# Two of the sixteen query weight tiles stay in SBUF, and the ring of gathered rows has eight slots in place of ten

## What is computed

```python
def block(xb):                                     # 128 tokens of 1024 values
    qh = (xb @ wq).reshape(128, 8, 2, 128)         # wq is 1024 x 2048
    s1 = einsum('thd,nd->thn', qh[:, :, 0], keys1)
    s2 = einsum('thd,nd->thn', qh[:, :, 1], keys2)
    v1, i1 = top_k(s1, 16); v2, i2 = top_k(s2, 16)
    cand = (v1[..., :, None] + v2[..., None, :]).reshape(128, 8, 256)
    sc, ci = top_k(cand, 16)
    e = take(i1, ci // 16) * 128 + take(i2, ci % 16)          # 128 tokens x 8 heads x 16 experts
    act = gelu(einsum('td,thkd->thk', xb, u_tab[e])) * softmax(sc)
    return einsum('thk,thkd->td', act, v_tab[e])
```

## Time and profile before

| | |
|---|---|
| median of 3 runs | 3160.18 us (3155.35 to 3163.76) |
| the profiled execution | 3159.13 us, its span 3157.3 us |
| PE busy | 2576.8 us (82%) |
| DVE busy | 2196.9 us (70%) |
| POOL busy | 1999.2 us (63%) |
| ACT busy | 691.8 us (22%) |
| DMA | 1212.72 MB in all, mean 384 GB/s; 1107.43 MB by the queue of the gathers, 102.80 MB by SP's |
| gathers | 1056 U, 1056 V (32 of them for the sample tokens) |

### The profile page before, as it was taken

The page is one execution under the profiler, slowest core; times in us unless marked ns, Lnnn a source line. Parts: engine busy times, 40 slices in busy tenths (PEclk is TensorE's granted clock), DMA queues, the critical chain, the costliest instruction groups (busy, mean ns, idle before and its releaser), DMA issues.

```text
span 3157.3 us, 39117 instructions
## 1 busy us (share of the span) xinstructions
PE 2576.8 (82%) x11988; PEld 1169.1 (37%) x11988; DVE 2196.9 (70%) x5635; ACT 691.8 (22%) x2526; POOL 1999.2 (63%) x2131
## 2 busy tenths in 40 slices
PE   7787989878987888778987888778987888777666
PEld 2553444234522453234522453234422453233111
DVE  2363887579856887579756987678756987678553
ACT  2121122112311122112311222112311232111112
POOL 0131667765777567765777567765777567766775
PEclk9888999878987899879987999878987999877566
DMA  7453999999999999999999999999999999999998
GB/s 268 136 205 116 411 387 405 419 419 385 404 413 419 416 384 419 419 419 385 412 415 419 410 388 414 419 416 368 418 412 419 414 387 414 419 419 378 417 419 356
DMA packets 339981, 1212.72 MB, mean 384 GB/s; under 512 B 41064, under 2 KB 41200, under 8 KB 339776
## 3 DMA queue, kind: packets, MB, share of 16 engines
q0 software_dynamic: 304128, 1107.43, 87.7%
q1 hardware_dynamic: 35648, 102.80, 8.4%
HBM read 1205.21 MB, written 4.87 MB: 383 GB/s over the span
## 4 chain that ended last, share of the span: by engine, by line
PE 33%; DMA 24%; DVE 22%; issue 11%; POOL 7%; ACT 3%; POOLq 0%; SPq 0%; DVEq 0%; ACTq 0%
PE bank L486 19%; DMA ring<-peer_v,idxv 17%; PE acc L486 14%; DVE ring L1496 8%; DMA ring<-peer_u,idx 7%; POOL ring L462 7%; DVE kw L1277 1%; DVE idxv L1329 1%; ACT xn L902 1%; DVE kw L1302 1%; DVE kw L1304 1%; DVE topi L1279 1%; DVE eh L1306 1%; DVE tops L1278 1%; DVE topi L1280 1%
## 5 line engine op out<-in xcount | busy, mean ns | idle before, releaser
L1496 DVE SCALAR_TENSOR_TENSOR ring<-ring,xcur 128x1024 f32<-128x1024 f32 x1056 | 1282.6, 1218 | 603.6 <-DMA ring<-peer_u,idx 596.7
L486 PE MATMUL acc<-ring,wv 128*32 128x512 f32 x4224 | 1304.9, 712 | 462.1 <-DMA ring<-peer_v,idxv 319.3
L462 POOL DMA_INDIRECT ring<-peer_u,idx x1056 | 1000.7, 948 | 685.7 <-issue 401.0
L462 POOL DMA_INDIRECT ring<-peer_v,idxv x1024 | 965.1, 942 | 409.4 <-issue 267.7
L486 PEld LDWEIGHTS acc<-ring,wv 128*32 128x32 f32 x4224 | 172.1, 115 | 1098.0 <-DMA ring<-peer_v,idxv 776.4
L486 PEld LDWEIGHTS bank<-xT,win 128*128 128x128 f32 (+1 forms) x2304 | 262.6, 182 | 104.7 <-issue 99.8
L486 PE MATMUL bank<-xT,win 128*128 128x128 f32 (+1 forms) x2304 | 293.0, 282 | 3.7 <-ACT xT L902 2.4
L902 ACT ACTIVATE wv<-rep,coefv 128x32 f32<-128x32 f32 x1024 | 264.4, 311 | 76.4 <-PE acc L486 74.5
L486 PE MATMUL bank<-win,xT 128*128 128x512 f32 (+3 forms) x368 | 184.0, 634 | 1.9 <-ACT xT L902 1.9
L486 PEld LDWEIGHTS bank<-xT,qk 128*128 128x128 f32 x1024 | 154.6, 239 | 65.6 <-issue 65.6
L486 PE MATMUL bank<-xT,qk 128*128 128x128 f32 x1024 | 167.8, 331 | 0.0
(11 more groups left out here) (231 smaller groups left out, 2181.5 us busy)
## 6 DMA issues: line engine op xcount, KB each, us to landing
qk<-wq SPq DMA_DIRECT2D x64, 512.0 KB, 6.6
t<-wq SPq DMA_DIRECT2D x64, 512.0 KB, 6.6
ring<-peer_u,idx POOLq DMA_INDIRECT x1056, 7.3
ring<-peer_v,idxv POOLq DMA_INDIRECT x1024, 7.2
win<-w_in SPq DMA_DIRECT2D x6, 2048.0 KB, 15.0
ring<-wq SPq DMA_DIRECT2D x16, 512.0 KB, 5.3
wout<-w_out SPq DMA_DIRECT2D x1, 4096.0 KB, 21.3
xn<-x_prompt SPq DMA_DIRECT2D x8, 512.0 KB, 8.4
```

The source lines that it names most:

```text
L462: pool.indirect_dma_start(out=ring[:, slot, :], out_offset=None, in_=(peer_u, peer_v)[which], in_offset=bass.IndirectOffsetOnAxis(ap=rows_ ...
L486: return nc.tensor.matmul(out, lhsT, rhs, start=start, stop=stop)
L1496: stt(row, row, 1.0, xcur[:, :], ALU.mult, ALU.mult, accum_out=dots[:, column(b, e):column(b, e) + 1]).then_inc(s_dot, 1)
```

## The change

Tiles 14 and 15 of `wq`, those of the last head, are loaded once, at the start, into a new tile `wq_kept`, and stay there. In the blocks SP loads tiles 0 to 13 alone. The new tile takes 8 KB of each partition, which are the two slots by which the ring is shorter.

```diff
-RING = 10
+RING = 8
+KEPT = 2
...
+        wq_kept = sb("wq_kept", [P, KEPT, CM, P])
...
             for ft in range(QUERY_SLOTS):
                 sp.dma_start(wq_s(ft), wq[ft]).then_inc(s_wq_s[ft], 16)
+            for half in range(KEPT):
+                sp.dma_start(wq_kept[:, half, :, :], wq[2 * PEER_HEADS - KEPT + half]).then_inc(s_wq_kept, 16)
             store_states(0, 0, 0)
...
             for b in range(BLOCKS - 1):
                 load_wq(b, range(12, 14))
                 load_x(b + 1, x_prompt[b * P + P:b * P + 2 * P, :])
-                load_wq(b, range(14, 16))
                 load_wq(b + 1, range(12))
                 store_y(b, y_prompt[b * P:b * P + P, :])
-            load_wq(BLOCKS - 1, range(12, 16))
+            load_wq(BLOCKS - 1, range(12, 14))
...
-                    pe.wait_ge(s_wq[half], b * 128 + 16 * head + 16)
+                    if ft >= 2 * PEER_HEADS - KEPT:
+                        pe.wait_ge(s_wq_kept, 16 * KEPT)
+                        tile = wq_kept[:, half, :, :]
+                    else:
+                        pe.wait_ge(s_wq[half], b * 16 * (PEER_HEADS - 1) + 16 * head + 16)
+                        tile = wq_buf[half]
                     for c in range(CM):
-                        last = mm(bank[2 + half][:, 0:P], wq_buf[half][:, c, :], xT[:, c, :], start=c == 0, stop=c == CM - 1)
+                        last = mm(bank[2 + half][:, 0:P], tile[:, c, :], xT[:, c, :], start=c == 0, stop=c == CM - 1)
```

More of the change, by code:

```diff
@@ L192, in program @@
         s_x = sem("s_x")
+        s_wq_kept = sem("s_wq_kept")
         s_wq = [sem("s_wq0"), sem("s_wq1")]
```

## The result

The changed kernel takes 3242.97 us in the median (3229.64 to 3249.95, 4 runs), before 3161.97 us (4 runs). The ratio is 1.0248, 95% interval 1.0229 to 1.0267: 81 us slower, where 40 were forecast. The profiled execution took 3240.89 us, its span 3239.1 us.

A forecast was written before the change was run, and what follows sets the result against it. Transfers were taken as the limit except in the heads, where DVE is. Terms of 2.5, 1.6 and 1.2 us made 5.3 a block, 37 for seven blocks, plus 2.5 for the last: 40 us slower, 3200 us, range 3162 to 3238.

The forecast's parts named there:

- The sign and the main mechanism: Whole kernel: 1.3% slower, since the shorter ring costs time and the removed loads give nothing back.
- The removed loads: Two loads fewer in each of eight blocks, before stretches with spare DMA time: taken as 0, bounds 0 and -20.0 us.
- A pause of POOL there can't be made good afterwards.: Away from weight loads, POOL back to back offers 423 GB/s, hardly more than the DMA engines take.
- the transfers are the limit outside the head slices: Outside the dips once a block, DMA engines nine tenths busy or more were read as the limit.
- The queue of 1.3 us: Gathers land 7.3 us after issue, 6.0 after a pause; the difference, queued transfers, covers that much of a pause.
- Term 1: End of each block's head: ring full behind DVE, then transfers limit; two slots fewer cost the full price, 2.5 us.
- Term 2: Mid-block stretch at 1943: PE's mixer piece makes POOL pause; eight slots lose 2.4 us, 1.6 more than ten.
- Term 3: Pauses ten slots hide wholly, as before 2086.18 and in the mixer: 1.2 us a block, bounds 0 and 7.5.
- The half price: Hidden pauses were charged half of one full price, 1.2 us a block, since weight loads lie beside them.
- The last block: Final block, without a mixer: only the end of its head costs, 2.5 us.
- the engines hang on each other: Rival: a late PE starves DVE in the head too; five places, 12.5 us a block, 100 us, 3260 us; chance 0.10.
- The checks named ahead: Changed profile: 7.3 MB less, waits above 417 us, landing under 7.3 us, 377 GB/s, loads near 360 us apart, deeper dips.

The follow-up runs named there:

- e2: Kernel before with ten slots, tiles 14 and 15 not loaded in the blocks: 3162.52 us, ratio 1.0006.
- e10: Kernel before with eight slots and no query weights loaded in the blocks, PE using columns of w_in instead: 3200.35 us, ratio 1.0113.
- e9: Kernel before, ten slots kept, with no query weights loaded in the blocks, PE using columns of w_in instead: 3118.68 us, ratio 0.9858.
- e1: Kernel before with eight slots instead of ten, all query weight tiles still loaded: 3249.34 us, ratio 1.0271.
- e3: Kernel before with its ten slots dealt by kind, four for U rows and six for V rows: 3202.54 us, ratio 1.0132.
- e5: Changed kernel with ACT making the V rows' weights up to three ticks earlier within each group of 16: 3234.52 us, ratio 1.0236.
- e8: Kernel before with seven slots instead of ten, all loads made: 3384.16 us, ratio 1.0714.

## Why the prediction was half right

**The sign and the main mechanism.** Both were right: the ring costs, the loads give nothing. The size was wrong: the measured 3243 us lie just outside the range of 3162 to 3238 us, twice as far from before as forecast.

**The removed loads, taken as 0.** Right. e2 shows it with the rest of the change left out.

**"A pause of POOL there can't be made good afterwards."** Right, and the main reading of the earlier trace rows: POOL's 1.24 us a gather leave no margin. e10 shows the price nearly unchanged (82 us for 90) with the loads gone. But the sentence before it, that the transfers are the limit outside the head slices, was too strong: e9 gets back 43 of 160 us. The busy share of nine tenths in the earlier trace rows doesn't tell POOL's pace from the engines' own. The queue of 1.3 us was read too small: the 6.0 us of the earlier trace rows are a median over 26 us of gathers, not the time after a pause. Of the gathers that went out after a pause of over 4 us in the trace of before, three have a landing on record: 4.1 to 4.3 us, all in the first 260 us of the kernel. A longer queue would cover more of a pause, so this error made the forecast larger, not smaller; it isn't what failed.

**Term 1, the end of the head, 2.5 us.** Right in size and place: 2.5 in the changed kernel, e1 and e3.

**Term 2, the stretch at 1943, 1.6 us.** Wrong in place: eight slots lose 0.1 us there, and the stretch 51 us later in the changed kernel has 414 GB/s, not fewer than 403. The pause at 1945.19 belonged to a short turn. It stands before the U gather of tick 82, which takes over the slot of a V, the ninth gather before it, and so waits for PE (`s_vsum`), though the trace puts its wait down to DVE. With eight slots no turn is short, and the U gather of tick 82 waits for a dot: its pause is 0.0 us in the mean where it was 1.2. Pauses of V gathers from tick 80 to 86, 0.9 us in all where there were 0.1, took its place. I had looked for pauses that were visible with ten slots and not asked which slot the gather waited for.

**Term 3, the pauses that ten slots hide, 1.2 us.** This is the step that failed, by its size. Measured is the rest of the block: 10.1 - 2.5 = 7.6 us for terms 2 and 3 together, 9.7 in e1, against 2.8 foreseen; the place of term 2 has 0.2 of it. The upper bound that I gave for this term alone, 7.5 us for three places at full price, would have been the right value. The half price rested on the loads of the weights lying beside these pauses. But the dearest stage, from tick 58 (1892 to 1932 us in the block shown), has no load beside it, and that from 98 (1996 to 2037 us) two, at 2028.8 and 2033.7. And the loads don't make pauses good: with none of them, in e10 against e9, eight slots cost 82 us where they cost 90 with them, and the stage from 98 costs 0.8 us without loads and 2.2 with them. The one pause that the term named, the 4.22 us before 2086.18, is a V gather's behind the first row of a group; its stage, from 130, loses nothing (-0.1). What the term should have counted is in the sorted table: POOL's pauses outside the head rise by 8.9 us a block, 3.7 of them behind DVE, 2.4 behind the first rows of the groups, 2.2 behind V rows 41 and 42. The last are shown by e5. The others are read from the traces, and no run takes them away. The trace had the numbers: a way round of 9.4 us for 9.9 leaves 0.5 us, and PE's pieces of mixer work of 2 us and more beside a 1 us sum were to be seen all through the block.

**The last block, 2.5 us.** It lost 10.5, though it has no mixer beside it. Its end of the head costs 3.4 us in this one execution (the stage from tick 42). Behind the head POOL's pauses are 12.7 us where they were 4.4, and 11.1 of them (4.0 before) stand behind the first two V rows of the groups, five of them 1.9 to 2.5 us long. So the turn from one group to the next costs without any mixer; the forecast had no term for it. This is one execution, and no run tries it.

**The rival "the engines hang on each other"** had 12.5 us a block and 100 us in all. Its size came nearest, e1 has 12.2 and 90. Its mechanism, PE starving DVE in the head, isn't what happened: from tick 18 to 42 nothing is lost.

**The checks named ahead.** SP's queue moved 95.46 MB against 102.80, as foreseen. POOL's waits rose above 417 us, to 532. The median to landing fell, to 6.6 us. The mean rate is 372 GB/s where 377 were named. The loads of `x_prompt` lie 358.9 us apart in the block shown and 361.7 in the mean of the last six, where 360 were named. The dip at 1943 didn't get deeper. The rate between the head and the next loads did not stay at 418.

## What to carry to other kernels

When buffers are traded for traffic, don't ask how full the DMA engines read, but who could issue more if there were room. Here the issuing engine runs back to back at nearly the rate of the engines, so a pause for lack of a slot is mostly lost for good, and one slot of 512 KB is worth about 45 us in 3160, while 8.4 MB less traffic beside a stretch that another engine limits is worth nothing that can be measured.

Work out the way round of a slot (issue to landing, use, release to next issue) against slots times pace. If what is left is smaller than the largest pieces of other work in the consumers' queues, count every such piece at full price, also those that cost nothing now. A wait that the present depth hides leaves no row on the issuing engine, but it has one on the consumer: PE waited 112.2 us for ACT's weights with ten slots already. Count also the periodic work, such as the weights for a new group every 16 rows, and look up in the code which slot a late gather waits for. And compare the last moments of equal rows (here the n-th dot) between traces: it names the places in a way that slices of the span can't.

## What the runs showed of the hardware that wasn't expected

Beside other gathers alone, with no weights loaded, a gather still takes 6.5 us in the median to land (e9), and with seven slots and all loads 6.2 us (e8's page). That isn't an empty way: where POOL had paused for over 4 us before, the six such gathers of e9 land 4.1 to 4.4 us after their issue (all in the first 260 us, with little other traffic). So by estimate some 3 us of the 7.3 with ten slots are time beside or behind other transfers, 0.8 of them that of the loads. And the releaser that a wait is put down to can be the wrong engine when two are done within a fraction of a microsecond: the pause at 1949.94 is put down to DVE, though that V gather waits for PE alone, and the one at 1945.19 of the kernel before, a U gather's, is put down to DVE too and waits for PE.
